# A two-block transformer kernel: the first attention in paired units with four-strip scores, and another way from its output projection into the first feed-forward

## The chip, the cores and the metric

One core of one Trainium2 chip. The metric is the device time in microseconds; lower is better. Engines: TensorE (PE), VectorE (DVE), ScalarE (ACT), GpSimd (POOL), SyncE (SP), which issues the weight loads.

## The reference, cut to what matters

Two transformer blocks on 512 tokens of width 1024, all float32. The change touches the first block's attention and the step from it to the feed-forward:

```python
# 8 heads, two maps each (p), dk = 32, dv = 64; slopes m = 2**-(h+1)
s = einsum('bqhpd,bkhpd->bphqk', q, k) * scale - m * |t - s|
p = softmax(s); w = p[:, 0] - lam * p[:, 1]
attn = rmsnorm(w @ v, g_subln) * (1 - lambda_init)     # mean over the 64 of a head
...
x = x + gt1 * (concat([attn, pool, conv]) @ w_out)
h = rmsnorm(x, g_ffn) * (1 + sc2) + sh2                # modulate
gate, up = split(h @ w_gate_up)
x = x + gt2 * ((silu(gate) * up) @ w_down)
```
`sh2`, `sc2`, `gt2` are columns of `silu(c) @ w_ada + b_ada`.

## The kernel before, in words

Activations lie transposed: width on 128 partitions, 8 chunks k, 512 tokens along the row. Each weight matrix comes in *slabs* of 128 output columns (1024 x 128): SyncE loads the slab into `w_raw` (two slots), ScalarE rounds it to `w_hi` (`split_high`, line 1039), VectorE takes the difference `w_lo` (`split_low`, 1442), TensorE does three matmuls per chunk with the split activations (`three`, lines 517 to 519; `chunk`, `part`, `whole`), 24 of 512 columns a slab. `w_used` counts slabs consumed; slab s+2's rounding waits for slab s. The order on every engine is written out by hand; semaphores carry the rest. PSUM banks have a fixed plan of turns (`plan`, `take`).

*First attention*, 32 units (8 heads x 4 blocks of 128 queries), loop over t. TensorE: scores of unit t, two calls (maps m) of 32 rows (line 635); half of one of the 14 slabs that remain of the input projection; transposes of unit t-2's weights (644); every second t the weighing of the values as `three` of 256 columns with `wt_hi`, `wt_lo`, `v1_hi`, `v1_lo`. VectorE: scores plus the head's ALiBi table with the minimum (1501, reads PSUM), then for unit t-1 reciprocal (1510), scaled second map (1511), combination (1512), for unit t-3 `wt_lo` (1519). ScalarE: exponentials with their sums (1156), `wt_hi` (1142), the output (1149), one ALiBi table a head (1081). GpSimd meanwhile computes, by row products and sums over `w_ada`, the modulation columns SH2 and SC2 (1844, 1846, 1848), and the pool and convolution branches. After the loop follow the pool branch's matmuls, half of two output slabs, the norm over each head (sum on TensorE, root on ScalarE, reciprocal on VectorE), the rest of the output projection.

*From output projection to feed-forward.* Each new chunk of x is squared on ScalarE (1183) and added up by GpSimd in `acc` (1923). After the eighth, TensorE sums over partitions (`token_sums`, 720), ScalarE and VectorE make 1/root, TensorE spreads it over all partitions (`spread`, 729). Then per chunk: `x_scaled` (VectorE, 1590, two buffers), `h_full` and `h_hi` (ScalarE, 1225), `h_lo` (VectorE, `low`, 1448). TensorE runs the gate slab over the eight chunks as they come, and then the up slab (`pair`). At the same time GpSimd makes the GT2 columns (`mod_products`). From then on a pair of gate and up slabs is one step n of 22: silu, product `t_hid`, `hid_hi`, `hid_lo` (1614).

*Second attention*: paired units already, with values weighed in plain float32, 64 columns wide, the two heads of a pair side by side (line 835). It is not touched.

## Time and profile before

| | |
|---|---|
| median of three runs | 1875.13 us (1870.35 to 1875.20) |
| the profiled execution, its own time | 1875.12 us |
| its span, first to last instruction | 1873.2 us |
| TensorE busy | 1765.0 us, 94% |
| VectorE / ScalarE / GpSimd busy | 884.4 / 637.3 / 299.6 us |
| mean granted TensorE clock | 0.970 of full speed |

Times of instructions are counted from the span's start. Matmuls are pipelined: a record's length is longer than the distance to the next one, so rates are read from starts. An idle time in square brackets names what ended it.

### The profile page before, as it was taken

The page shows a single profiled execution, that of the slowest core. Times are in us where ns is not written, and L with a number is a line of the kernel's source. Part 1 is how long each engine was busy: PE and PEld are TensorE (multiplying, and loading weights), DVE is VectorE, ACT ScalarE, POOL GpSimd, SP SyncE. Part 2 cuts the span into 40 slices and gives each one's busy share as a digit, 9 for nine tenths or more (in the row PEclk, how much of TensorE's full clock was granted, in tenths as well). Part 3 has the DMA queues.
Part 4 walks back from the last instruction along what each step waited for, and adds up shares of the span by engine and source line. Part 5 has one row for each costly group of instructions (what it writes and reads, how often), then busy time and mean ns, then how long its engine had stood idle before and what let it go on. Part 6 is the DMA issues. An engine that isn't in the chain of part 4 may idle for free.

```text
span 1873.2 us, 22878 instructions
## 1 busy us (share of the span) xinstructions
PE 1765.0 (94%) x8047; PEld 1399.8 (75%) x8047; DVE 884.4 (47%) x1258; ACT 637.3 (34%) x1088; POOL 299.6 (16%) x237
## 2 busy tenths in 40 slices
PE   5699989699999999999999999899899999999998
PEld 2566667478888887888888887566678888888886
DVE  5678884643333333444443332555545544444322
ACT  3245553422232223222232222354544433233222
POOL 6286621630000112100001012001100200000000
PEclk9799999699999999999999999999999999999999
DMA  9343311333333333533333327111223333333331
GB/s 344 94 135 91 90 34 48 110 112 100 93 98 97 93 98 91 141 93 101 91 108 113 97 87 146 53 50 54 57 79 101 90 91 100 98 92 108 97 96 70
DMA packets 299469, 184.54 MB, mean 99 GB/s; under 512 B 14859, under 2 KB 285703, under 8 KB 299399
## 3 DMA queue, kind: packets, MB, share of 16 engines
q1 hardware_dynamic: 290336, 157.30, 28.6%
q0 software_dynamic: 7424, 25.29, 4.9%
q10 hardware_dynamic: 1656, 1.25, 0.2%
q8 instruction: 33, 0.54, 0.1%
q14 instruction: 20, 0.16, 0.0%
HBM read 180.67 MB, written 6.36 MB: 100 GB/s over the span
## 4 chain that ended last, share of the span: by engine, by line
PE 75%; issue 5%; DVE 3%; ACT 1%; DMA 1%; POOL 1%; DVEq 0%; POOLq 0%; SPq 0%; ACTq 0%
PE psum L517 24%; PE psum L519 24%; PE psum L518 24%; PE psum L862 1%; PE psum L835 1%; DMA w_raw<-in_w_in 1%; PE psum L878 1%; DVE w_lo L1442 1%; DVE h_lo L1448 1%; ACT w_hi L1039 1%; POOL acc L1923 1%; PE psum L729 0%; ACT wt L1325 0%; DVE p L1738 0%; DVE p L1756 0%
## 5 line engine op out<-in xcount | busy, mean ns | idle before, releaser
L517 PE MATMUL psum<-h_hi,w_hi 128*128 128x512 f32 x1480 | 593.0, 401 | 25.1 <-DVE h_lo L1448 11.0
L518 PE MATMUL psum<-h_lo,w_hi 128*128 128x512 f32 x1480 | 582.5, 394 | 0.0
L519 PE MATMUL psum<-h_hi,w_lo 128*128 128x512 f32 x1480 | 582.0, 393 | 0.0
L1442 DVE TENSOR_TENSOR w_lo<-w_raw,w_hi 128x1024 fp32r<-128x1024 f32 (+1 forms) x258 | 365.6, 1417 | 392.1 <-ACT w_hi L1039 388.6
L517 PEld LDWEIGHTS psum<-h_hi,w_hi 128*128 128x128 f32 x1480 | 281.5, 190 | 125.0 <-issue 38.4
L1039 ACT ACTIVATE w_hi<-w_raw 128x1024 fp32r<-128x1024 f32 (+1 forms) x258 | 286.5, 1110 | 161.5 <-PE psum L519 146.5
L519 PEld LDWEIGHTS psum<-h_hi,w_lo 128*128 128x128 f32 x1480 | 281.6, 190 | 60.2
L518 PEld LDWEIGHTS psum<-h_lo,w_hi 128*128 128x128 f32 x1480 | 282.0, 191 | 56.4 <-issue 0.5
L519 PE MATMUL psum<-hid_hi,w_lo 128*128 128x512 f32 x528 | 210.7, 399 | 0.0
L518 PE MATMUL psum<-hid_lo,w_hi 128*128 128x512 f32 x528 | 208.1, 394 | 0.0
L517 PE MATMUL psum<-hid_hi,w_hi 128*128 128x512 f32 x528 | 207.1, 392 | 0.0
L1923 POOL TENSOR_TENSOR acc<-acc,sq 128x512 f32<-128x512 f32 x48 | 65.9, 1373 | 818.7 <-ACT sq L1183 817.8
L1245 ACT ACTIVATE hid_hi<-t_hid 128x512 f32 (+1 forms) x66 | 41.9, 635 | 283.1 <-DVE t_hid L1610 283.1
L518 PEld LDWEIGHTS psum<-hid_lo,w_hi 128*128 128x128 f32 x528 | 99.1, 188 | 25.8
L517 PEld LDWEIGHTS psum<-hid_hi,w_hi 128*128 128x128 f32 x528 | 99.1, 188 | 23.5
L519 PEld LDWEIGHTS psum<-hid_hi,w_lo 128*128 128x128 f32 x528 | 99.1, 188 | 22.8
L1610 DVE TENSOR_TENSOR t_hid<-psum,t_silu 128x512 f32<-128x512 f32 x66 | 45.6, 692 | 141.8 <-PE psum L519 141.8
L1241 ACT ACTIVATE t_silu<-t_gate 128x512 f32<-128x512 f32 x44 | 27.8, 632 | 160.2 <-DVE t_gate L1605 160.2
L1614 DVE TENSOR_TENSOR hid_lo<-t_hid,hid_hi 128x512 f32 (+1 forms) x66 | 47.0, 712 | 64.8 <-ACT hid_hi L1245 64.8
L1848 POOL TENSOR_TENSOR acc<-acc,sq 128x1024 f32<-128x1024 f32 x28 | 75.6, 2699 | 2.2
L1156 ACT ACTIVATE p<-p,stat 128x512 f32<-128x512 f32 x64 | 45.8, 717 | 61.9 <-DVE stat L1501 61.8
L1605 DVE TENSOR_TENSOR t_gate<-psum,rs 128x512 f32<-128x512 f32 x44 | 30.4, 692 | 71.7 <-PE psum L519 71.6
(241 smaller groups left out, 1667.3 us busy)
## 6 DMA issues: line engine op xcount, KB each, us to landing
w_raw<-in_w_in SPq DMA_DIRECT2D x50, 512.0 KB, 3.9
w_raw<-in_w_gate_up SPq DMA_DIRECT2D x44, 512.0 KB, 3.8
w_raw<-in_ffn_w_gate SPq DMA_DIRECT2D x44, 512.0 KB, 3.8
w_raw<-in_ffn_w_up SPq DMA_DIRECT2D x44, 512.0 KB, 3.8
w_raw<-in_ffn_w_down SPq DMA_DIRECT2D x32, 704.0 KB, 4.6
sq<-in_w_ada POOLq DMA_DIRECT2D x32, 512.0 KB, 4.2
w_raw<-in_w_down SPq DMA_DIRECT2D x16, 704.0 KB, 4.6
ada_w<-in_w_ada SPq DMA_DIRECT2D x4, 2048.0 KB, 21.0
```

What stands on the lines that cost most here:

```text
L517: pe.matmul(o, a_hi, b_hi, start=start, stop=False)
L518: pe.matmul(o, a_hi, b_lo, start=False, stop=False)
L519: return pe.matmul(o, a_lo, b_hi, start=False, stop=stop)
L1039: act.activation(w_hi[:, s % 2, 0:n], w_raw[:, s % 2, 0:n], ACT.Identity).then_inc(w_high, 1)
L1156: act.activation(p1[:, t % 3, m, :], p1[:, t % 3, m, :], ACT.Exp, bias=stat[:, t % 3, m:m + 1], scale=-1.0, accum_out=stat[:, t % 3, 2 + m ...
L1245: act.activation(hid_hi[:, slot_of(n, i), :], t_hid[:, :], ACT.Identity).then_inc(hid_high, 1)
L1442: dve.tensor_tensor(w_lo[:, s % 2, 0:n], w_raw[:, s % 2, 0:n], w_hi[:, s % 2, 0:n].bitcast(F32), ALU.subtract).then_inc(w_ready, 1)
L1605: dve.tensor_tensor(t_gate[:, :], psum[:, b, :], rs[:, :], ALU.mult).then_inc(gate_scaled, 1)
L1610: dve.tensor_tensor(t_hid[:, :], psum[:, b, :], t_silu[:, :], ALU.mult).then_inc(hid_set, 1)
L1614: dve.tensor_tensor(hid_lo[:, at, :], t_hid[:, :], hid_hi[:, at, :].bitcast(F32), ALU.subtract)\
L1848: last = pool.tensor_tensor(mod_acc, mod_acc, ada_row[:, k % 2, :], ALU.add)
L1923: pool.tensor_tensor(acc[:, m, :], acc[:, m, :], sq[:, n, m, :], ALU.add).then_inc(summed, 1)
```

## The change

The first attention has 16 units, each a pair of heads and a block of queries. Scores are four calls in four strips of 32 rows, into four banks, issued back to back; all are reduced against one shared distance table `dist` (q carries the reciprocal slope by `qscale`, and the exponential's scale and the small `least` multiply it back). The combination is not normalized: `combine` weighs the second map with -lam times the ratio of sums, and the head norm takes the missing factor by `el` = EPS x sum squared. Weights and values stay plain float32 (`wt`, `v1`) and are weighed in the second attention's manner. p1 has two buffers of four maps instead of three of two. On VectorE `combine(t-1)` stands ahead of unit t's reductions.

Into the feed-forward: slab 29 is split before the root; GpSimd adds seven squares and TensorE sums the eighth from `sq`; `x_scaled` (four buffers) takes `scale2` as well, `h_full` is gone, `h_lo` comes from `x_scaled` plus shift less `h_hi`; gate and up slab run together, chunk by chunk (`first_pair`); GpSimd's GT2 products wait for `hid_ready` 2. The pool branch's second part on ScalarE and VectorE stands at t = 17. The diff, cut:

```diff
         (t_gate, t_silu, t_hid), _ = region(OVER, BIG, [(n, [P, T], F32) for n in ("t_gate", "t_silu", "t_hid")])
-        (x_scaled, h_full), _ = region(OVER + 3 * T * BYTES, BIG, [(n, [P, 2, T], F32) for n in ("x_scaled", "h_full")])
+        (x_scaled,), _ = region(OVER + 3 * T * BYTES, BIG, [("x_scaled", [P, 4, T], F32)])
...
-        (q1, k1, v1_hi, v1_lo, wt_hi, wt_lo, o1, p1, alibi, dist), at1 = region(BIG, BIG_END, [
-            ("q1", [P, 4, T], F32), ("k1", [P, 4, T], F32), ("v1_hi", [P, TT, T], F32R),
-            ("v1_lo", [P, TT, T], F32R), ("wt_hi", [P, 2, TT, 2 * P], F32R),
-            ("wt_lo", [P, 2, TT, 2 * P], F32R), ("o1", [P, 4, T], F32), ("p1", [P, 3, 2, T], F32),
-            ("alibi", [P, 2, 2 * T - P], F32), ("dist", [P, 2 * T - P], F32)])
+        (q1, k1, v1, wt, o1, p1, dist), at1 = region(BIG, BIG_END, [
+            ("q1", [P, 4, T], F32), ("k1", [P, 4, T], F32), ("v1", [P, TT, T], F32),
+            ("wt", [P, 2, TT, 2, 2 * P], F32), ("o1", [P, 4, T], F32), ("p1", [P, 2, 2, 2, T], F32),
...
-                    for m in range(2):
-                        b = take(("s1", t, m))
-                        r = DH * (h % 2) + DQ1 * m
-                        pe.matmul(psum[:, b, :], q1[r:r + DQ1, c, P * i:P * i + P], k1[r:r + DQ1, c, :],
-                                  start=True, stop=True).then_inc(filled[b], 1)
...
-                u = t - 2
-                if 0 <= u < UN1:
-                    pe.wait_ge(combined, u + 1)
...
+                    for j in range(2):
+                        for m in range(2):
+                            take(("s1", t, j, m))
+                    for j in range(2):
+                        for m in range(2):
+                            b = bank_of(("s1", t, j, m))
+                            r = DH * j + DQ1 * m
+                            pe.matmul(psum[:, b, :], q1[r:r + DQ1, c, P * i:P * i + P], k1[r:r + DQ1, c, :],
+                                      start=True, stop=True).then_inc(filled[b], 1)
+                if t < N_MIX1:
+                    part(S_MIX1 + t, 0, 2)
+                u = t - 1
+                if u >= 0:
...
+                    for j in range(2):
+                        pe.wait_ge(combined, 2 * u + j + 1)
+                        b = take(("t1", u, j))
+                        for kt in range(TT):
+                            last = pe.transpose(psum[:, b, P * kt:P * kt + P], p1[:, u % 2, j, 0, P * kt:P * kt + P],
+                                                ident[:, :])
...
-                    wait_emptied(pe, ("t1", 2 * g))
-                    wait_emptied(pe, ("t1", 2 * g + 1))
+                    for j in range(2):
+                        wait_emptied(pe, ("t1", u, j))
...
+                            d = DH * (2 * c + j)
+                            last = pe.matmul(psum[DH * j:DH * j + DH, b, 0:2 * P], v1[:, kt, d:d + DH],
+                                             wt[:, g % 2, kt, j, :], start=kt == 0, stop=kt == TT - 1)
                     last.then_inc(filled[b], 1)
...
-            token_sums("ffn0", "out1")
+            b = take(("sum", "ffn0"))
+            for part_, ready in ((acc[:, 0, :], (summed, SUM0 + KD - 1)), (sq[:, 1, 0, :], (squared, KD))):
+                pe.wait_ge(*ready)
+                for i in range(TT):
+                    last = pe.matmul(psum[:, b, i:i + 1], part_[:, P * i:P * i + P], mean_d,
...
-                pair(0)
+                def first_pair():
+                    for n, key in enumerate(("gate", "up")):
+                        await_slab(s0 + n)
+                        take((key, 0, 0))
+                    for k in range(KD):
+                        pe.wait_ge(h_ready, h0 + k + 1)
+                        for n, key in enumerate(("gate", "up")):
+                            last = three(psum[:, bank_of((key, 0, 0)), :], *tile(s0 + n, k), *hs[k], k == 0, k == KD - 1)
+                            if k == KD - 1:
+                                last.then_inc(w_used, 1)
+                if f == 0:
+                    first_pair()
+                else:
+                    pair(0)
                 pair(1)
...
+            def exps(t, j):
+                c, i = t // 4, t % 4
+                col = 8 * i + 2 * c + j
+                act.wait_ge(least_set, 2 * t + j + 1)
+                for m in range(2):
+                    at = 2 * j + m
+                    act.activation(p1[:, t % 2, j, m, :], p1[:, t % 2, j, m, :], ACT.Exp,
+                                   bias=quad[:, t % 2, 4 + at:5 + at], scale=-(2.0 ** -(2 * c + j + 1)),
+                                   accum_out=lsum[:, m, col:col + 1]).then_inc(expd, 1)
...
-                u = t - 3
+                if t < N_MIX1:
+                    split_high(S_MIX1 + t + 1)
+                if t >= 3 and t % 2:
+                    keep_o1((t - 3) // 2)
...
+                if t < UN1:
+                    exps(t, 0)
+                u = t - 1
...
+                    for j in range(2):
+                        b = wait_filled(act, ("t1", u, j))
+                        act.activation(wt[:, g % 2, :, j, P * (u % 2):P * (u % 2) + P],
+                                       psum[:, b, :].rearrange("p (k q) -> p k q", k=TT), ACT.Copy)\
+                           .then_inc(emptied[b], 1)
...
+                    exps(t, 1)
...
                 act.activation(q1[:, c, :], o1[:, c, :], ACT.Square).then_inc(o_squared, 1)
-            b = wait_filled(act, "sub_sum")
-            act.activation(rsub[:, :], psum[:, b, 0:32], ACT.Sqrt, bias=eps).then_inc(emptied[b], 1)
+            wait_emptied(act, "sub_sum")
+            act.activation(rsub[:, :], rsub[:, :], ACT.Sqrt).then_inc(sub_root, 1)
...
...
                 act.wait_ge(scaled_x, k + 1)
-                if k >= 2:
-                    act.wait_ge(h_ready, 8 * GEN["ffn0"] + k - 1)
-                for dst, done_ in ((h_full[:, k % 2, :], h_whole), (h_hi[:, k, :], h_high)):
-                    act.activation(dst, x_scaled[:, k % 2, :], ACT.Identity, bias=modc[:, SH2 + k:SH2 + k + 1],
-                                   scale=scale2[:, k:k + 1]).then_inc(done_, 1)
+                act.activation(h_hi[:, k, :], x_scaled[:, k % 4, :], ACT.Identity, bias=modc[:, SH2 + k:SH2 + k + 1])\
+                   .then_inc(h_high, 1)
...
-                dve.wait_ge(v_high, i + 1)
-                dve.tensor_tensor(v1_lo[:, i, :], psum[:, b, :], v1_hi[:, i, :].bitcast(F32), ALU.subtract)\
-                   .then_inc(emptied[b], 1)
             split_low(5)
...
+            def combine(u):
+                c, i = u // 4, u % 4
+                at = 8 * i + 2 * c
+                dve.wait_ge(expd, 4 * u + 4)
+                done(dve.reciprocal(quad[:, u % 2, 8:10], lsum[:, 1, at:at + 2]))
+                dve.scalar_tensor_tensor(out=quad[:, u % 2, 10:12], in0=lsum[:, 0, at:at + 2], scalar=neg_lam,
+                                         in1=quad[:, u % 2, 8:10], op0=ALU.mult, op1=ALU.mult).then_inc(ratio_set, 1)
+                dve.wait_ge(ratio_set, u + 1)
+                for j in range(2):
+                    dve.scalar_tensor_tensor(out=p1[:, u % 2, j, 0, :], in0=p1[:, u % 2, j, 1, :],
+                                             scalar=quad[:, u % 2, 10 + j:11 + j], in1=p1[:, u % 2, j, 0, :],
+                                             op0=ALU.mult, op1=ALU.add).then_inc(combined, 1)
...
+                for m in range(2):
+                    wait_emptied(dve, ("s1", t, j, m))
+                dve.tensor_scalar(quad[:, t % 2, 4 + 2 * j:6 + 2 * j], quad[:, t % 2, 2 * j:2 * j + 2],
+                                  2.0 ** -(2 * (t // 4) + j + 1), None, ALU.mult).then_inc(least_set, 1)
...
+                if 1 <= t <= UN1:
+                    combine(t - 1)
+                if t < UN1:
+                    i = t % 4
+                    for j in range(2):
+                        if t >= 2:
+                            wait_filled(dve, ("t1", t - 2, j))
+                        for m in range(2):
+                            b = wait_filled(dve, ("s1", t, j, m))
+                            dve.tensor_tensor_reduce(p1[:, t % 2, j, m, :], psum[:, b, :],
+                                                     dist[:, T - P - P * i:2 * T - P - P * i], 1.0, 3e38,
+                                                     ALU.add, ALU.min, quad[:, t % 2, 2 * j + m:2 * j + m + 1])\
+                               .then_inc(emptied[b], 1)
+                            if j == 1 and m == 0:
+                                least(t, 0)
+                    least(t, 1)
+                if t < N_MIX1:
+                    split_low(S_MIX1 + t + 1)
...
-                    done(dve.reciprocal(st[:, 4:6], st[:, 2:4]))
-                    done(dve.tensor_scalar(p1[:, n, 1, :], p1[:, n, 1, :], st[:, 5:6], neg_lam, ALU.mult, ALU.mult))
-                    dve.scalar_tensor_tensor(out=p1[:, n, 0, :], in0=p1[:, n, 0, :], scalar=st[:, 4:5],
-                                             in1=p1[:, n, 1, :], op0=ALU.mult, op1=ALU.add).then_inc(combined, 1)
...
-                if 0 <= u < UN1:
-                    b = bank[("t1", u)]
-                    at = slice(P * (u % 2), P * (u % 2) + P)
-                    dve.wait_ge(wt_high, u + 1)
-                    dve.tensor_tensor(wt_lo[:, u // 2 % 2, :, at], psum[:, b, :].rearrange("p (k q) -> p k q", k=TT),
-                                      wt_hi[:, u // 2 % 2, :, at].bitcast(F32), ALU.subtract).then_inc(emptied[b], 1)
...
+            dve.scalar_tensor_tensor(out=el[:, :], in0=lsum[:, 0, :], scalar=EPS, in1=lsum[:, 0, :],
+                                     op0=ALU.mult, op1=ALU.mult).then_inc(sub_added, 1)
             split_low(S_OUT1 + 1)
-            wait_emptied(dve, "sub_sum")
+            dve.wait_ge(sub_added, 1)
+            b = wait_filled(dve, "sub_sum")
+            dve.tensor_tensor(rsub[:, :], psum[:, b, 0:32], el[:, :], ALU.add).then_inc(emptied[b], 1)
+            dve.wait_ge(sub_root, 1)
             dve.reciprocal(rsub[:, :], rsub[:, :]).then_inc(sub_scaled, 1)
...
+            split_low(S_GU[0] + 1)
...
-                    if k >= 2:
-                        dve.wait_ge(h_high, 8 * GEN["ffn0"] + k - 1)
-                    dve.tensor_tensor(x_scaled[:, k % 2, :], x[:, k, :], psum[:, b, :], ALU.mult).then_inc(scaled_x, 1)
+                    if k >= 4:
+                        dve.wait_ge(h_ready, 8 * GEN["ffn0"] + k - 3)
+                    dve.scalar_tensor_tensor(out=x_scaled[:, k % 4, :], in0=x[:, k, :], scalar=scale2[:, k:k + 1],
+                                             in1=psum[:, b, :], op0=ALU.mult, op1=ALU.mult).then_inc(scaled_x, 1)
                 if k:
                     j = k - 1
-                    dve.wait_ge(h_whole, j + 1)
-                    low(h_lo[:, j, :], h_full[:, j % 2, :], h_hi[:, j, :], 8 * GEN["ffn0"] + j)
+                    dve.wait_ge(scaled_x, j + 1)
+                    dve.wait_ge(h_high, 8 * GEN["ffn0"] + j + 1)
+                    dve.scalar_tensor_tensor(out=h_lo[:, j, :], in0=x_scaled[:, j % 4, :],
+                                             scalar=modc[:, SH2 + j:SH2 + j + 1], in1=h_hi[:, j, :].bitcast(F32),
+                                             op0=ALU.add, op1=ALU.subtract).then_inc(h_ready, 1)
...
             wait_filled(pool, ("mod", SC2 // KD))
-            sums("out1", None)
+            pool.memset(acc[:, 0, :], 0.0).then_inc(summed, SUM0)
+            pool.wait_ge(summed, SUM0)
+            for n in range(KD - 1):
+                pool.wait_ge(squared, n + 1)
+                pool.tensor_tensor(acc[:, 0, :], acc[:, 0, :], sq[:, n % 2, 0, :], ALU.add).then_inc(summed, 1)
+                pool.wait_ge(summed, SUM0 + n + 1)
+            pool.wait_ge(hid_ready, 2)
             mod_row(GT2 // KD, 0)
-            wait_filled(pool, ("sum", "ffn0"))
             mod_products(GT2 // KD)
             wait_filled(pool, ("mod", GT2 // KD))
-            sums("down0", "ffn0", 2)
+            sums("down0", None, 2)
```

## Rows read from the trace of the kernel before

**Rows 1.** The page: busy time by engine, and the group of slab roundings.
```profile
PE 1765.0 (94%) x8047; PEld 1399.8 (75%) x8047; DVE 884.4 (47%) x1258; ACT 637.3 (34%) x1088; POOL 299.6 (16%) x237
...
L1039 ACT ACTIVATE w_hi<-w_raw 128x1024 fp32r<-128x1024 f32 (+1 forms) x258 | 286.5, 1110 | 161.5 <-PE psum L519 146.5
```
**Rows 2.** Busy time of each engine (instructions) in five stretches, granted clock, DMA.
```profile
105.10:264.20 159.10, 150.24 (x728) 106.14 (x728) 142.67 (x239) 84.82 (x180) 102.39 (x65) 0.97 0.31 91
176.00:218.20 42.20, 38.31 (x189) 27.19 (x188) 40.97 (x60) 21.25 (x46) 38.34 (x21) 0.98 0.41 125
243.00:264.20 21.20, 20.73 (x105) 14.81 (x104) 18.23 (x37) 11.03 (x24) 6.73 (x6) 1.00 0.17 51
...
354.30:376.60 22.30, 13.17 (x25) 6.67 (x25) 22.17 (x15) 13.39 (x17) 20.73 (x13) 0.50 0.30 95
395.90:439.40 43.50, 43.50 (x193) 36.05 (x192) 15.35 (x16) 12.53 (x16) 0.00 (x0) 1.00 0.34 97
```
**Rows 3.** TensorE in time order, two units of the first attention: start us, us.
```profile
171.55 1.13 PE L635 MATMUL psum<-k,q 32*128 32x512 f32 x4
...
172.60 0.50 PE L517 MATMUL psum<-h_hi,w_hi 128*128 128x512 f32 x1
...
175.46 0.60 PE L644 MATMUL psum<-ident,p 128*128 128x128 f32 x4
...
175.99 1.13 PE L635 MATMUL psum<-k,q 32*128 32x512 f32 x4
...
181.86 1.13 PE L635 MATMUL psum<-k,q 32*128 32x512 f32 x4
```
**Rows 4.** TensorE in time order, weighing of values in the second attention.
```profile
1213.04 2.38 PE L835 MATMUL psum<-wt,vb 128*64 128x256 f32 x24
```
**Rows 5.** Time order, units 28 and 29 of the first attention.
```profile
264.22 1.13 PE L635 MATMUL psum<-k,q 32*128 32x512 f32 x4
...
265.52 0.69 DVE L1501 CUSTOM_DVE_ANT_0 p<-psum,alibi 128x512 f32<-128x512 f32 x1 [1.95 <-PE psum L635]
...
266.13 0.68 DVE L1501 CUSTOM_DVE_ANT_0 p<-psum,alibi 128x512 f32<-128x512 f32 x1
266.25 0.72 ACT L1156 ACTIVATE p<-p,stat 128x512 f32<-128x512 f32 x1 [1.54 <-DVE stat L1501]
...
266.94 0.55 DVE L1511 TENSOR_SCALAR p<-p,stat,small 128x512 f32<-128x512 f32 x1
...
267.80 0.60 ACT L1142 ACTIVATE wt_hi<-psum 128x512 fp32r<-128x512 f32 x1
```
**Rows 6.** VectorE's groups, and one line's spread, 176 to 218; last, 243 to 264.
```profile
L1511 DVE TENSOR_SCALAR p<-p,stat,small 128x512 f32<-128x512 f32 x7 | 11.4, 1630 | 0.3
...
L1512 DVE SCALAR_TENSOR_TENSOR p<-p,stat 128x512 f32<-128x512 f32 x7 | 8.8, 1253 | 0.2
...
L1512 DVE SCALAR_TENSOR_TENSOR p<-p,stat x7: 752/753/2747, 180.8 to 217.2; 128x512 f32<-128x512 f32 x7
...
L1442 DVE TENSOR_TENSOR w_lo<-w_raw,w_hi 128x1024 fp32r<-128x1024 f32 x2 | 2.4, 1224 | 1.1 <-ACT w_hi L1039 1.1
```
**Rows 7.** TensorE in time order, start of the second output slab.
```profile
288.82 0.50 PE L517 MATMUL psum<-h_hi,w_hi 128*128 128x512 f32 x1 [0.57 <-DVE w_lo L1442]
```
**Rows 8.** Time order, from the last output slab into the feed-forward.
```profile
346.54 1.87 PE L720 MATMUL psum<-small,acc 128*128 128x1 f32 x8 [3.08 <-POOL acc L1923]
...
351.08 1.29 DVE L1590 TENSOR_TENSOR x_scaled<-x_res,psum 128x512 f32<-128x512 f32 x2 [2.17 <-PE psum L729]
...
376.59 0.80 PE L517 MATMUL psum<-h_hi,w_hi 128*128 128x512 f32 x1 [1.66 <-DVE w_lo L1442]
...
380.34 0.39 PE L517 MATMUL psum<-h_hi,w_hi 128*128 128x512 f32 x1
...
390.34 0.50 PE L517 MATMUL psum<-h_hi,w_hi 128*128 128x512 f32 x1 [0.99 <-DVE w_lo L1442]
...
395.92 0.39 PE L517 MATMUL psum<-h_hi,w_hi 128*128 128x512 f32 x1
```

More of the change, by code:

```diff
@@ L183, in program @@
         stat = place("stat", [P, 3, 8])
+        quad = place("quad", [P, 2, 16])
+        lsum = place("lsum", [P, 2, 32])
+        el = place("el", [P, 32])
+        qscale = place("qscale", [P, 4])
         rsub = place("rsub", [P, 32])
@@ L649, in _ @@
+                if t < N_MIX1:
+                    part(S_MIX1 + t, 1, 2)
+                if u >= 0 and u % 2:
+                    g = u // 2
+                    c = g // 2
                     if g == 0:
```

187 lines of the change are left out of this document (73 added, 114 removed).

## The prediction, made before the changed kernel was run

> **What bounds the kernel now.** I read the page first, then the busy time by stage, then the two changed stretches instruction by instruction. TensorE is busy 94% of the span [rows 1], so a gain must come from fewer TensorE microseconds or from its waits. The stage view [rows 2] separates three cases. In 395.9 to 439.4 eight slabs take 43.5 us: 5.44 us a slab, 0.227 us a matmul of 512 columns; only fewer matmuls would help there, and the change takes none. In the first attention (105.1 to 264.2, 28 of 32 units with 14 slabs) TensorE is busy 150 of 159 us and VectorE 143. While GpSimd works (176 to 218) TensorE has 38.3 of 42.2 us and VectorE is full (41.0); when GpSimd is nearly quiet (243 to 264) TensorE is full. So this loop has two limits taking turns. In 354.3 to 376.6, the change into the feed-forward, TensorE is busy 13.2 of 22.3 us at a granted clock of 0.50 (1.2 GHz) and VectorE is full.
>
> **The loop: TensorE's side.** Before, an even unit lasts 4.44 us (171.55 to 175.99): 1.05 us scores, 2.86 us half a slab, 0.53 us transposes with their switch [rows 3]. The odd unit behind it, with 12 small matmuls for the values, lasts 5.9 us (to 181.86). Two units: 10.3 us. After, one iteration does two units' work:
> - Scores: four calls in four 32-row strips. Two calls in two strips, two passes each, are four records in 1.13 us, and TensorE goes on after 1.05 [rows 3]. No row has four strips. Bounds: 1.05 us (all together) and 2.1 us (two at a time). I take 1.05, because two strips show no cost of sharing.
> - Slab 5.44 us, eight transposes 0.9 us, switches 0.4 us: 7.8 us.
> - Weighing of values, every second iteration: plain float32, 64 columns wide, two heads side by side. The same form in the second attention takes 2.38 us for 24 records, which are 12 passes a head, eight of 256 and four of 128 columns [rows 4]: 2560 columns a head, 0.93 ns each. Eight passes of 256 are 1.9 us.
> Mean iteration: 7.8 + 1.9/2 = 8.7 us against 10.3 for the same work.
>
> **The loop: VectorE and ScalarE's side.** The scaled product, `wt_lo` and `v1_lo` go away, and the ALiBi tables on ScalarE. But combine(t-1) stands before unit t's score reductions, and p1 has two buffers, so a ring forms. From the first reduction of unit t [rows 5]: three reductions at 0.61 us (265.52 to 266.13) and the small `least`, 2.1; two exponentials 1.55 (266.25 to 267.80), 3.65; two copies of transposed weights at under 0.6 us, 4.8; two exponentials, 6.35; reciprocal and product with their waits 0.45; two products of 0.75 us overlapping slightly, 1.35; so 8.15 us until unit t+1's reductions start. Undisturbed, this hides behind TensorE's 8.7.
> GpSimd disturbs it. In 176 to 218 the combining product has a median of 0.75 us, undisturbed, but a mean of 1.25, and its neighbour a mean of 1.63 [rows 6] instead of 0.55 [rows 5]: 1.6 us extra for a pair. Two such products remain in the ring, so a disturbed iteration takes 9.75 us. GpSimd's work is not reduced: 102 us busy in the old loop [rows 2], of some 131 us in the new: share 0.78. Mean ring: 8.15 + 0.78 x 1.6 = 9.4 us, above 8.7: the ring becomes the bound. The Trainium skill ("TensorEngine Tiling (Array Packing)", PSUM Bottleneck) warns of this: after row tiling, emptying PSUM may be the bottleneck. The trace agrees in kind: four reductions, 2.4 us, follow 1.05 us of scores.
> What is queued in this ring: TensorE's transposes wait for combine; behind them stand the second half slab and the weighing; a late weighing also holds the next scores. Over two iterations these shift by some 2 us but add nothing to 9.4.
>
> **Ends of the loop.** Before: scores of unit 28 at 264.22, second output slab's first matmul at 288.82 [rows 5, 7], 183.7 us from the loop's start at 105.1. After: first reduction at 105.1 + 1.3 = 106.4 (1.3 is 264.22 to 265.52); 14 iterations, 131.6; one more ring, 8.2; then combine 8.2, transposes 0.6 and last copy 0.9 with handshakes, weighing 1.9, pool matmuls 1.9 (four passes of 512 columns at the scores' rate), and from their first half on ScalarE's two copies, two roundings, the slab split of 1.1 [rows 1] and VectorE's difference of 1.2 [rows 6], 4.1 beyond them: 17.7. That is 263.9, or 24.9 us earlier. The drain alone is worse than before (27 us from iteration 14 against 24.6), since no slab covers the two last rings. The added hop in the sub-layer norm (VectorE adds `el` before ScalarE's root) costs 0.3. Result: 24.6 us saved. The added hop is estimated from the reciprocal's place in that chain. The eight more memsets lie in VectorE's wait for the first DMA; uncovered they are one-column writes, well under 0.5 us each.
>
> **The change into the feed-forward.** Squares of the last column go to TensorE directly, so eight sum matmuls start where GpSimd's last addition started: 1.3 us sooner than 346.54, and scaling starts at 349.9 instead of 351.08 [rows 8]. The split of slab 29 fits into that chain's waits (cover: the 4.5 us in which VectorE and ScalarE hold only root and reciprocal; uncovered 2.3 us). The old stretch took 22.3 us for eight k, 2.8 each, with three matmuls a k and GpSimd busy throughout [rows 2]. The new k has two products on VectorE, 1.4 us undisturbed, one rounding on ScalarE, and feeds six matmuls, 1.36 us at full clock. x_scaled has four buffers, so VectorE waits for no one after the first. First matmul at 352.4. From a low clock the old kernel needed 3.75 us for nine back-to-back matmuls (376.59 to 380.34) before the rate rose: 1.7 us lost. End of both slabs: 352.4 + 48 x 0.227 + 1.7 = 365.0. Now the price: both slabs are released together, so slab 30 waits for the gate's silu, some 0.6 like the copies of [rows 5], the split 1.1 and the difference 1.2, less 0.5 since the gate ends first: first matmul at 367.4. Slab 31's split hides behind slab 30. Slab 32 starts at 378.3, against 395.92 before: 17.6 us saved.
> The GT2 products move to where `hid_ready` is 2, some 380, and run for about 41 us as before (some 351 to 392: GpSimd is busy 20.7 of 22.3 us with them in [rows 2], and `w_lo` still suffers at 390), now under the steady stream. There the old kernel shows one such stall: slab 31 waits 0.99 us for `w_lo` [rows 8]. Four pairs of 10.9 us fall into it: 4 us lost, with bounds 0 (each difference falls between GpSimd's operations) and 8. GpSimd's queue holds nothing else due before the down projection. The Trainium skill ("SBUF — State Buffer", SBUF: two separate sides) speaks against this move: a VectorE operation with two SBUF inputs is blocked for the whole of a GpSimd operation that reads SBUF. The trace agrees, by the 0.99 us of slab 31.
>
> **Sum.** 24.6 + 17.6 - 4 = 38.2 us. The profiled execution took 1875.12 us (span 1873.2), equal to the median 1875.13, so the forecast is 1837 us.
>
> **Rivals.**
> 1. *TensorE keeps both stretches.* GpSimd's work hardly hits the ring, since only two products are exposed, and no stalls: 14 x 0.7 = 10 and 4 us more, 1823. For it: the median of 0.75 even in the disturbed stretch [rows 6]. Against: the mean. 12%.
> 2. *Strips run two at a time.* TensorE's iteration becomes 9.75, every iteration is at both limits, about 10.1: +10, 1847. For it: no row with four strips. 10%.
> 3. *Low clock through the first pair.* 48 matmuls at 0.42 (nine in 3.75 us) instead of 0.227, less the 1.7: +8, 1845. For it: 354 to 377 ran at 0.50 throughout. Against: TensorE waited for 9 of those 22 us; back-to-back work from 376.59 raised the clock. 9%.
> 4. *GpSimd's lock at its worst.* Both products last until GpSimd's operation ends, 2.75 each, the longest there [rows 6]: ring 12.3 in ten of 14 iterations, +26, 1863. Stalls may double. 7%.
> 5. *The other side: the ring's waits let the clock fall inside the loop.* At 1.2 GHz an iteration's TensorE work is some 16 us, 6.6 more than the forecast; from six such iterations the whole gain is gone, at ten it is 1903, slower than before. For it: the old loop's mean of 0.97 says that it fell at times. Against: that mean came with TensorE 94% busy, and I expect 93%. 3%.
> 6. *The removed matmuls were covered by waits already*, and the transition gain alone comes: 1861. 3%.
> Forecast 56%.
>
> **How the numbers follow.** Within the forecast: loop bounds 8.7 to 10 us an iteration (-10, +8), stalls 0 to 8 us, first pair +-3: 1826 to 1850. The range for 8 in 10 takes in most of rivals 1 to 3 and stops short of 4 and 6: 1822 to 1857. A difference of 0.3% (5.6 us) is about what this measurement can tell. Only rival 5 and the far ends of 4 and 6 together come near 1869: faster 0.96, within 0.3% 0.02, slower 0.02.
>
> **What would show it.** Right: `p` scores as eight records in about 1.15 us; starts of `psum<-k,q` 9 to 10 us apart, shorter where GpSimd is idle; TensorE waiting for `p` of the combining line; second output slab near 264; six matmuls a k near 1.4 us; a 2.4 us gap before slab 30; GpSimd's `acc` products after the second pair, with `w_lo` far above its 1.2 us and stalls near 1 us beside them. Wrong: scores of 2 us, iterations over 11 us, granted clock 0.50 across the loop or the whole first pair, or stalls of over 2 us a pair.

## The result, and where the microseconds went

The changed kernel takes 1856.8 us (median of four runs, 1855.3 to 1857.9) against 1875.2 for the kernel before on the same chip: a ratio of 0.9908, 95% interval 0.9897 to 0.9920, so 17 us or 0.9% faster. The forecast was 1837, with a range of 1822 to 1857. The profiled execution took 1855.3 us, its span 1853.5, 19.7 less than the span before.

The page's row of busy time, to be read beside [rows 1]:
```profile
PE 1734.3 (94%) x7991; PEld 1377.6 (74%) x7991; DVE 854.1 (46%) x1232; ACT 618.1 (33%) x1064; POOL 303.4 (16%) x236
```
TensorE has 30.7 us less to do, and only 19.7 of them left the span: 11 us turned into waits. Four stretches of the changed kernel, busy time by engine as in [rows 2], say where:
```profile
105.10:254.40 149.30, 126.35 (x696) 89.76 (x688) 129.71 (x220) 73.70 (x168) 105.08 (x64) 0.99 0.32 96
254.40:283.30 28.90, 17.06 (x73) 9.61 (x72) 12.35 (x32) 15.45 (x34) 0.00 (x0) 0.70 0.00 1
343.20:366.20 23.00, 18.24 (x73) 14.64 (x74) 14.56 (x20) 10.08 (x13) 0.00 (x0) 0.88 0.18 52
371.60:415.00 43.40, 41.74 (x181) 33.55 (x180) 23.44 (x16) 12.52 (x16) 34.75 (x21) 1.00 0.60 177
```
The first is 14 iterations of the new loop. TensorE idles 23 of 149 us at full clock and VectorE 20: neither is full, which is what a ring of waits looks like. GpSimd is busy 105 us. From the first reduction of unit 0 (105.97) to that of unit 15 (263.92) the mean distance is 10.5 us; 9.4 was forecast. The single distances go with GpSimd: 11.8 to 15.2 us in the five iterations in which it is busy for some 11 us or more, 8.6 and 7.8 us in the two in which it is busy for under 2 (the last two, without any GpSimd work, run into the drain). Since each unit's reductions stand behind the combining products of the unit before, no distance can be shorter than the ring: undisturbed, the ring is at most 7.8 us long, where 8.15 was forecast. The last stretch runs under GT2's products, where TensorE is no longer full.

The same points of the kernel in both traces (us from the span's start; before from [rows 3, 5, 7, 8], and the last from the same two traces):

| point | before | after | gained so far | forecast |
|---|---|---|---|---|
| second output slab | 288.82 | 283.31 | 5.5 | 24.9 |
| scaling of the feed-forward starts | 351.08 | 343.19 | 7.9 | 25.8 |
| first matmul of slab 32 | 395.92 | 371.60 | 24.3 | 42.2 |
| end of the span | 1873.2 | 1853.5 | 19.7 | 38.2 |

The difference stands in the first line: the loop gained 5.5 us instead of 24.9. The steps behind it came out nearly as forecast, within 1.5 us each.

**The loop, operation by operation.** VectorE's lines in the loop of the changed kernel: number, shortest, median and longest duration in ns. L1520 is `least`, L1508 the ratio, L1512 the two combining products, L1507 the reciprocal, L1475 `w_lo`:
```profile
L1520 DVE TENSOR_SCALAR quad<-quad x32: 155/420/2283, 107.8 to 266.6; 128x2 f32<-128x2 f32 x32
L1508 DVE SCALAR_TENSOR_TENSOR quad<-lsum,small,quad x16: 220/774/1593, 114.3 to 270.1; 128x2 f32<-128x2 f32 x16
L1512 DVE SCALAR_TENSOR_TENSOR p<-p,quad x32: 737/754/2979, 115.5 to 271.0; 128x512 f32<-128x512 f32 x32
L1507 DVE RECIPROCAL quad<-lsum x16: 153/166/168, 114.1 to 269.9; 128x2 f32<-128x2 f32 x16
L1475 DVE TENSOR_TENSOR w_lo<-w_raw,w_hi x15: 1210/1212/1226, 112.5 to 282.0; 128x1024 fp32r<-128x1024 f32 x15
```
An operation on two columns needs 0.155 us and takes up to 2.28. Its neighbour, a reciprocal of the same size, takes 0.15 to 0.17 every time. Over all their instances, the time beyond the shortest is 16.6 us for `least`, 9.1 for the ratio and 22.4 for the combining products: 48 us (called blocked time below), of which the forecast had counted 17.5 (14 iterations at 1.25), and only on L1512. That is 3.0 us a unit; with a ring of at most 7.8 it makes 10.8, an estimate to be held against the 10.5 measured. One stretch shows what they wait for and how that reaches TensorE, all engines in time order (start, duration; in brackets the idle time before and what ended it):
```profile
124.25 2.11 DVE L1520 TENSOR_SCALAR quad<-quad 128x2 f32<-128x2 f32 x1
...
124.42 1.91 POOL L1896 TENSOR_TENSOR sq<-sq,cact 128x1024 f32<-128x1024 f32 x1
...
126.28 1.21 DVE L1475 TENSOR_TENSOR w_lo<-w_raw,w_hi 128x1024 fp32r<-128x1024 f32 x1
126.39 0.72 ACT L1140 ACTIVATE p<-p,quad 128x512 f32<-128x512 f32 x1 [0.33 <-DVE quad L1520]
126.40 3.32 POOL L1898 TENSOR_TENSOR acc<-acc,sq 128x1024 f32<-128x1024 f32 x1
...
127.82 0.57 ACT L1120 ACTIVATE k<-psum 128x512 f32<-128x512 f32 x1
...
128.15 1.59 DVE L1508 SCALAR_TENSOR_TENSOR quad<-lsum,small,quad 128x2 f32<-128x2 f32 x1
...
128.54 0.47 PE L522 MATMUL psum<-h_hi,w_hi 128*128 128x512 f32 x1 [2.73 <-ACT k L1120]
...
129.78 3.30 DVE L1512 SCALAR_TENSOR_TENSOR p<-p,quad 128x512 f32<-128x512 f32 x2
...
130.61 1.91 POOL L1896 TENSOR_TENSOR sq<-sq,cact 128x1024 f32<-128x1024 f32 x1
...
132.60 2.74 POOL L1898 TENSOR_TENSOR acc<-acc,sq 128x1024 f32<-128x1024 f32 x1
...
133.13 0.66 PE L653 MATMUL psum<-ident,p 128*128 128x128 f32 x4 [1.15 <-DVE p L1512]
```
`least` ends at 126.36, when GpSimd's multiplication ends (126.33). `w_lo` starts right there, ahead of GpSimd's next operation, and now GpSimd waits: its addition lasts 3.32 us, where the one at 132.60 lasts 2.74 and the one at 104.88, with nothing of VectorE beside it, 2.38. The ratio then waits until 129.74, that addition's end (129.72), and the two combining products take 3.30 us instead of 1.4, the second one held until the multiplication at 130.61 is over. There are two ways from here to TensorE. The short one is the last row: transposes wait for the combining product. The long one is at 128.54: a late `least` makes the exponentials late; the copy of the slab's result out of its only PSUM bank is queued behind them on ScalarE, and the next half slab waits 2.73 us for that bank.

Does TensorE's lateness come back into the ring? All waits of ScalarE and then of VectorE in the 14 iterations say hardly (us in total, times, longest):
```profile
ACT p L1140 <- DVE quad L1520: 71.9, 19, 8.0
```
```profile
DVE quad L1507 <- ACT p L1140: 12.6, 13, 2.0
DVE p L1547 <- PE psum L643: 6.1, 1, 6.1
DVE y_side L1536 <- PE psum L524: 2.6, 1, 2.6
DVE conv_u L1531 <- PE psum L524: 1.0, 1, 1.0
```
The one wait for scores (L643) is that of unit 0, before the loop. From unit 1 to unit 14 no reduction waits for scores and ScalarE never waits for TensorE; 3.6 us before two products of the convolution branch are all that VectorE waits for it. VectorE and ScalarE set the pace, and TensorE follows.

**TensorE's own side** was as forecast. Scores in four strips, a weighing, the last rings and the second output slab:
```profile
176.41 1.14 PE L643 MATMUL psum<-k,q 32*128 32x512 f32 x8
177.49 0.50 PE L522 MATMUL psum<-h_hi,w_hi 128*128 128x512 f32 x1
...
138.13 1.95 PE L670 MATMUL psum<-wt,v 128*64 128x256 f32 x16 [1.58 <-ACT wt L1185]
...
261.93 1.86 PE L643 MATMUL psum<-k,q 32*128 32x512 f32 x8
...
271.14 1.97 PE L653 MATMUL psum<-ident,p 128*128 128x128 f32 x8 [6.33 <-DVE p L1512]
273.84 3.52 PE L670 MATMUL psum<-wt,v 128*64 128x256 f32 x16 [0.73 <-issue]
...
283.31 0.49 PE L522 MATMUL psum<-h_hi,w_hi 128*128 128x512 f32 x1 [0.33 <-DVE w_lo L1475]
```
Eight records in 1.14 us, four strips together, the next matmul 1.08 after the first: four calls cost what two cost in [rows 3]. The weighing takes 1.95. In the drain the granted clock falls (0.70 over the second stretch above, 0.56 from 270 to 278) and the same weighing takes 3.52.

**The change into the feed-forward**, TensorE and the scaling in time order, to be read beside [rows 8]:
```profile
337.23 0.95 PE L751 MATMUL psum<-small,acc 128*128 128x1 f32 x8
...
343.19 1.41 DVE L1635 SCALAR_TENSOR_TENSOR x_scaled<-x_res,scale,psum 128x512 f32<-128x512 f32 x2 [1.81 <-PE psum L743]
...
345.75 0.77 PE L522 MATMUL psum<-h_hi,w_hi 128*128 128x512 f32 x1 [2.68 <-DVE h_lo L1641]
...
360.54 0.50 PE L522 MATMUL psum<-h_hi,w_hi 128*128 128x512 f32 x1 [2.21 <-DVE w_lo L1475]
...
371.60 0.39 PE L522 MATMUL psum<-h_hi,w_hi 128*128 128x512 f32 x1
```
From the scaling's start to slab 32 it is 28.4 us, as forecast (349.9 to 378.3), and 44.8 before. The scaling itself starts 5.6 us after the last residual (337.57) instead of 7.5 (343.63).

### The profile page after: what moved, and what is told of

It reads as the page before. It is cut to its first block, busy times and chain, and to the rows that moved or that the text cites. A ratio compares the mean times of both kernels' runs of the same rounds, so it can differ in the third digit from the quotient of the medians.

```text
span 1853.5 us, 22726 instructions
## 1 busy us (share of the span) xinstructions
PE 1734.3 (94%) x7991; PEld 1377.6 (74%) x7991; DVE 854.1 (46%) x1232; ACT 618.1 (33%) x1064; POOL 303.4 (16%) x236
## 3 DMA queue, kind: packets, MB, share of 16 engines
q10 hardware_dynamic: 1656, 1.25, 0.2%
## 4 chain that ended last, share of the span: by engine, by line
PE 81%; DVE 10%; ACT 4%; issue 3%; DMA 2%; ACTq 0%; DVEq 0%; SPq 0%
PE psum L522 26%; PE psum L524 25%; PE psum L523 25%; DVE p L1512 2%; ACT p L1140 1%; DVE w_lo L1475 1%; DVE first_acc L1449 1%; DVE p L1547 1%; PE psum L869 1%; DMA ada_w<-in_w_ada 1%; ACT w_hi L1073 1%; PE psum L896 1%; DVE quad L1520 1%; DMA w_raw<-in_w_in 1%; PE psum L912 1%
## 5 line engine op out<-in xcount | busy, mean ns | idle before, releaser
L1475 DVE TENSOR_TENSOR w_lo<-w_raw,w_hi 128x1024 fp32r<-128x1024 f32 (+1 forms) x258 | 357.6, 1386 | 388.0 <-ACT w_hi L1073 384.6
L1974 POOL TENSOR_TENSOR acc<-acc,sq 128x512 f32<-128x512 f32 x40 | 55.6, 1391 | 736.4 <-ACT sq L1215 735.5
L1140 ACT ACTIVATE p<-p,quad 128x512 f32<-128x512 f32 x64 | 45.6, 715 | 80.5 <-DVE quad L1520 80.5
```

What stands on the lines that cost most here:

```text
L1140: act.activation(p1[:, t % 2, j, m, :], p1[:, t % 2, j, m, :], ACT.Exp, bias=quad[:, t % 2, 4 + at:5 + at], scale=-(2.0 ** -(2 * c + j + 1 ...
L1475: dve.tensor_tensor(w_lo[:, s % 2, 0:n], w_raw[:, s % 2, 0:n], w_hi[:, s % 2, 0:n].bitcast(F32), ALU.subtract).then_inc(w_ready, 1)
L1974: pool.tensor_tensor(acc[:, m, :], acc[:, m, :], sq[:, n, m, :], ALU.add).then_inc(summed, 1)
```

## Experiments

All ratios are against the kernel before, timed in the same job; the changed kernel's is 0.9908. "Keep" is when ScalarE keeps the last weighed block of values (277.40 in the changed kernel, 286.04 before), which closes the loop and its drain. It and the blocked time were counted in each trace over the lines named above.

**1 and 2: GpSimd made quiet, in the changed kernel and in the one before.** Left out are seven of eight multiplications and the additions for two vectors; the rest of GpSimd's work stays.
```
 for k in range(KD):
     ...
     pool.wait_ge(row_landed[k % 2], rows_loaded[k % 2])
+    if j in (SH2 // KD, SC2 // KD):
+        if k == KD - 1:
+            last = pool.tensor_tensor(mod_acc, ada_row[:, 1, :], cact[...], ALU.mult)
+        continue
```


> The changed kernel, but GpSimd multiplies only the last of the eight row blocks for each of the two vectors that it computes in the first attention (SH2 and SC2); the other seven multiplications and their additions are left out, their transfers stay. So both vectors, and the output, have other values. Theory A (GpSimd's SBUF operations block VectorE's small and wide operations in the ring): the blocked microseconds, 48 over the three lines, nearly vanish; the loop's mean distance falls from 10.6 to 8.7 to 9.0 us, and the kernel becomes 22 to 28 us faster than the changed one, near 1832. Theory B (the order of the ring, combine before the next reductions with two buffers, binds even without GpSimd): distance stays at 10 us or more, under 8 us gained. Theory C (TensorE's clock): distance stays where the granted clock was low, gain under 5 us.

> The kernel before, with the same operations of GpSimd left out (other values in SH2, SC2 and the output). It is the control. Theory A: the old loop has a third p1 buffer and more of TensorE's work to hide behind, so it gains less than the changed one, some 8 to 14 us against 22 to 28. If it gains as much as the changed one, GpSimd's disturbance was no worse for the new ring than for the old one, and A doesn't explain the shortfall.

Measured: 1831.2 us, ratio 0.9772 (0.9751 to 0.9793), so 26 us faster than the changed kernel; keep 254.34. The kernel before, treated alike: 1865.6, ratio 0.9956 (0.9941 to 0.9971), 8 us faster. The lines of `least` and of the combining products, and 124.9 us of the loop by engine, in the first:
```profile
L1520 DVE TENSOR_SCALAR quad<-quad x32: 154/169/657, 108.5 to 243.5; 128x2 f32<-128x2 f32 x32
...
L1512 DVE SCALAR_TENSOR_TENSOR p<-p,quad x32: 737/750/1870, 112.2 to 247.9; 128x512 f32<-128x512 f32 x32
...
105.10:230.00 124.90, 122.20 (x688) 87.88 (x688) 92.74 (x217) 75.25 (x169) 40.50 (x37) 1.00 0.37 116
```
TensorE now is the bound: 122.2 of 124.9 us busy for the 14 slabs, so 8.7 us of work in an iteration of 8.9, and 8.7 is the forecast's figure for its side. Blocked time fell from 48 to 12 us. GpSimd's operations for the two vectors take 26 us from the new kernel and 8 from the old: the new order is more exposed to the same work. It isn't that there was little to block before. Counted alike (15.0 us on line 1511, 11.6 on 1512, 10.0 on `w_lo`), the old loop had 37 us of blocked time against 48. Taking 28 of the 37 away gave back 8 us there; taking 36 of the 48 away gave back 26 here. Between the two quiet kernels lie 34 us, near the 38 that were forecast for the loud ones. Theory A holds in both numbers, C falls (nothing was done to the clock, which is 1.00 here and was 0.99), and B as the only cause falls.

**3 and 4: the two parts of the change apart.** Experiment 3 is the kernel before with the diff's edits from the sum matmuls of `ffn0` on (`x_scaled`, `first_pair`, the GT2 products' place); experiment 4 has all the others.

> The kernel before with only the edits of the change into the feed-forward (sum matmuls of the last column directly, both slabs together, one rounding per k on ScalarE, GT2 products later). If the parts are additive as the two traces suggest: 14 to 16 us faster than before, about 1860. If the attention's part was worth nothing or less: 18 us, all of the change's gain.

> The kernel before with only the edits of the first attention. Additive as the traces suggest: 5 to 7 us faster, about 1869. If this part was in truth worth what the forecast said and the transition nothing: 18 or more. If it is a loss that the transition covers: no change or slower.

Measured: the transition alone 1857.4 us, ratio 0.9919 (0.9896 to 0.9942), 15 us faster. The attention alone 1871.7 over ten runs, ratio 0.9990 (0.9979 to 1.0001): 2 us, and not to be told from nothing by the 0.3% bound. 5 to 7 us were expected, after the 5.5 us that the traces above show at the second output slab; that figure rather overstates this part. The two add up to the whole. So a loop with 24 us less of TensorE's work in it (1740.9 us busy in experiment 4's trace, 1765.0 before) was worth about 2 us, and the transition made nearly all of the gain.

**5: `least` on ScalarE.**
```
-least(t, 0)
 ...
-least(t, 1)                           # on VectorE
 ...
+act.activation(quad[:, t % 2, 4 + 2*j:6 + 2*j], quad[:, t % 2, 2*j:2*j + 2],
+               ACT.Copy, scale=2.0 ** -(2*c + j + 1)).then_inc(least_set, 1)
```


> The changed kernel with `least` (the product of two columns, 32 of them) on ScalarE instead of VectorE, in front of the exponentials. Theory A as the trace tells it (tiny operations wait for GpSimd too): 16.6 us of blocked time leave VectorE, 32 operations of about 0.25 us enter ScalarE's side of the ring; if the block doesn't move to the next operation, the loop gets 6 to 12 us shorter. Rival A2 (the port is held anyway, so the block moves on to the ratio and the combining products): their mean rises and the kernel stays within 3 us. Theory B: within 3 us as well, but with their means unchanged.

Measured: 1850.5 us, ratio 0.9872 (0.9856 to 0.9889), 6 us faster; keep 269.95. ScalarE's form of it, and the two VectorE lines (here L1479 is `w_lo`, L1512 the ratio) that stand next:
```profile
L1139 ACT ACTIVATE quad<-quad 128x2 f32<-128x2 f32 x32 | 6.4, 200 | 65.1 <-DVE quad L1551 65.1
```
```profile
L1479 DVE TENSOR_TENSOR w_lo<-w_raw,w_hi x15: 1212/1216/2942, 107.8 to 275.7; 128x1024 fp32r<-128x1024 f32 x15
...
L1512 DVE SCALAR_TENSOR_TENSOR quad<-lsum,small,quad x16: 220/846/2152, 110.7 to 262.5; 128x2 f32<-128x2 f32 x16
```
On ScalarE it takes 0.200 us every time. But `w_lo`, never blocked in the changed kernel's loop, now goes up to 2.94 us, and the ratio's longest grows from 1.59 to 2.15: of the 16.6 us that left with `least`, 8.3 came back on the next operations. `w_lo` had been free only because `least` had waited in front of it. Both A and A2 hold, each for half.

**6 and 7: a third buffer and another order, alone and with `least` on ScalarE.** The edit in short:
```
-("p1", [P, 2, 2, 2, T], F32)            +("p1", [P, 3, 2, 2, T], F32)
 # VectorE, iteration t
-combine(t - 1); reductions of t; w_lo    +reductions of t; w_lo; combine(t - 1)
 # TensorE and ScalarE
-u = t - 1   # unit transposed, copied    +u = t - 2
```


> The changed kernel with a third p1 buffer; VectorE reduces unit t before it combines unit t-1, and TensorE transposes unit t-2. Everything else stays, GpSimd's work too. Theory B (the ring's order lets each blocked microsecond through to the end): distance falls from 10.6 to 9.0 to 9.6 us, since blocked time fills VectorE's idle time; the end one iteration later takes back 2 to 4; 12 to 20 us faster, about 1840. Theory A alone (VectorE is full with blocked time whatever the order): under 5 us. Theory C (clock): under 3 us.

> Both edits: the third buffer with the other order, and `least` on ScalarE. If both causes count: 3 to 8 us faster than the skewed ring alone. If the skewed ring has already hidden the blocked time behind TensorE: within 2 us of it. If ScalarE's two small operations come late for the exponentials: slower than it by 2 to 4.

Measured: alone 1849.5 us, ratio 0.9861 (0.9844 to 0.9877), 8 us faster, keep 270.05. Together 1839.6 us, ratio 0.9811 (0.9794 to 0.9827), 17 to 18 us faster than the changed kernel, keep 259.58. Alone it gained about half of what theory B wanted (12 to 20 us); together they gained more than was expected (3 to 8 us beyond experiment 6, measured 10). The loop of experiment 6 by engine:
```profile
105.10:249.30 144.20, 129.93 (x672) 92.80 (x665) 127.88 (x213) 73.19 (x165) 102.33 (x64) 0.93 0.33 99
```
The granted clock is 0.93 where it was 0.99 in the changed kernel, and TensorE is busy 129.9 us with fewer matmuls than took 126.4 there. Part of what this experiment lacks may be the clock; nothing here takes the two apart, and the profiled execution was its slowest run (1852.3). TensorE's waits in the loop, the changed kernel first, then the one with both edits (us in total, times, longest):
```profile
PE psum L653 <- DVE p L1512: 9.9, 9, 2.2
PE psum L522 <- ACT k L1120: 5.5, 2, 2.7
```
```profile
PE psum L670 <- ACT wt L1189: 4.5, 3, 3.0
PE psum L653 <- DVE p L1516: 1.8, 3, 1.4
```
The waits for the combining product nearly go. Blocked time does not (44.6 us, against 48): it is now borne beside TensorE's work. In the version with the third buffer alone, `least` still stands in front of `w_lo` and of the exponentials, and the waits for ScalarE's copies behind them stay; that would be the part that `least` on ScalarE then takes. This is a reading, not shown: the 3 to 4 us by which 17 to 18 exceeds the sum of 8 and 6 are as much as single runs of one kernel differ (2 to 4 us), and the clock differs too (0.97 in experiment 7's loop).

**8: GT2's products where they were before.**
```
-pool.wait_ge(hid_ready, 2)
 mod_row(GT2 // KD, 0)
+wait_filled(pool, ("sum", "ffn0"))
 mod_products(GT2 // KD)
```


> The changed kernel, but GpSimd's GT2 products start when the sum matmuls of the scaling have run, as before the change, and not after the first gate-and-up pair. Forecast's reason: the products then lie under the eight k of the transition, where VectorE issues two products a k; the six matmuls a k stretch from 1.4 towards 2.5 us, 5 to 9 us lost there, and 2.9 us of stalls later come back in part: 3 to 7 us slower than the changed kernel. Rival: the transition has room, so the earlier start costs nothing and saves up to 2.9 us.

Measured: 1862.4 us, ratio 0.9930 (0.9910 to 0.9950), 4 to 6 us slower than the changed kernel (its profiled execution, 1864.5, 9 us slower). Its transition in time order:
```profile
345.88 2.70 POOL L1898 TENSOR_TENSOR acc<-acc,sq 128x1024 f32<-128x1024 f32 x1
346.27 0.73 DVE L1635 SCALAR_TENSOR_TENSOR x_scaled<-x_res,scale,psum 128x512 f32<-128x512 f32 x1
...
346.93 2.20 DVE L1641 SCALAR_TENSOR_TENSOR h_lo<-x_scaled,modc,h_hi 128x512 fp32r<-128x512 f32 x1
```
Both products are 512 wide and have the same form. `x_scaled` has one input in PSUM and takes 0.73 us in the middle of GpSimd's addition; `h_lo` has both in SBUF, takes 2.20 and ends 0.55 us after GpSimd's addition (348.58). A k takes 2.8 us here, as in the kernel before. From the scaling to slab 30 it is 29.5 us instead of 17.4; under the steady stream behind it TensorE waits no more. The move was worth its price.

**9: GpSimd's operations in halves.**
```
-done(pool.tensor_tensor(ada_row[:, k % 2, :], ...)); last = pool.tensor_tensor(mod_acc, ...)
+for a in range(2):
+    at = slice(D // 2 * a, D // 2 * (a + 1))
+    ...
+    done(pool.tensor_tensor(ada_row[:, k % 2, at], ...))
+    last = pool.tensor_tensor(mod_acc[:, at], ...)
```


> The changed kernel, but each of GpSimd's multiplications and additions for SH2 and SC2 is two of 512 columns instead of one of 1024: the same data, half the length of one operation, twice the number of gaps. Theory A by length (a blocked operation waits for the GpSimd operation that is running): a wait is about half as long, so of the 48 us of blocked time some 15 to 24 go, and the kernel becomes 8 to 15 us faster than the changed one; the longest `least` falls from 2.3 to about 1.3 us. Rival A3 (after each wait GpSimd's next half blocks again, so the sum of waits is what counts): within 3 us, since GpSimd's busy time grows a little. If GpSimd's own chain gets so long that its vectors come late for TensorE: slower.

Measured: 1846.5 us, ratio 0.9855 (0.9834 to 0.9876), 10 us faster; keep 268.36. `least` and GpSimd's additions in it:
```profile
L1520 DVE TENSOR_SCALAR quad<-quad x32: 155/540/1379, 107.2 to 257.4; 128x2 f32<-128x2 f32 x32
```
```profile
L1902 POOL TENSOR_TENSOR acc<-acc,sq 128x512 f32<-128x512 f32 x27 | 40.5, 1498 | 2.1
```
The longest wait falls with the length of GpSimd's operation, 2.28 to 1.38 us, and the longest combining product from 2.98 to 1.85. Blocked time goes from 48 to 36, somewhat less than expected. GpSimd's work for the two vectors did not shrink, it grew from 65 to 73 us: this ties the wait to the length of one GpSimd operation, not to how much GpSimd does.

**10 to 12: edits together, and the new order without GpSimd.**

> Third buffer with the other order, `least` on ScalarE, and GpSimd's SH2 and SC2 operations in halves. If the causes add: 3 to 8 us faster than the version with the first two (1839.6), about 1834. If the other order has already hidden what is left of the waits: within 2 us of it.

> As the one before, and the GT2 operations under the second and later gate-and-up pairs in halves too. Theory: the differences `w_lo` there wait for half an operation less; of the 2.9 us of stalls 1.5 to 2.9 come back. Rival: a difference in progress delays GpSimd and is delayed the same way, nothing changes (within 1 us).

> Third buffer with the other order, `least` on ScalarE, and GpSimd's operations for SH2 and SC2 left out as in the first experiment (other values in both vectors and the output). It says what the order of the ring costs without GpSimd. Theory A: it cost nothing, so this is within 3 us of the first experiment (1831.2, distance 8.9). Theory B: 5 us or more below it, since TensorE no longer waits for `combined` at all.

Measured: 10, 1841.2 us, ratio 0.9821 (0.9803 to 0.9840), no better than experiment 7: the halves add nothing to the other two edits. 11, 1838.0, ratio 0.9803 (0.9785 to 0.9821), 3 us below 10. Its `w_lo` under the GT2 products, after the changed kernel's over the same slabs:
```profile
L1475 DVE TENSOR_TENSOR w_lo<-w_raw,w_hi x10: 1212/1686/3416, 374.3 to 425.0; 128x1024 fp32r<-128x1024 f32 x10
```
```profile
L1479 DVE TENSOR_TENSOR w_lo<-w_raw,w_hi x10: 1226/1924/2504, 361.0 to 409.3; 128x1024 fp32r<-128x1024 f32 x10
```
The longest is 0.9 us shorter, and that suffices: from the first matmul of one slab pair to that of the next it is 10.88 us undisturbed; the four disturbed pairs of the changed kernel took 11.65, 11.83, 11.78 and 11.18, here 11.11, 10.94, 10.88 and 10.88. Experiment 11 beats both kernels: 2.0% faster than the kernel before. 12, 1826.5, ratio 0.9746 (0.9724 to 0.9768): 5 us below experiment 1. So the two edits are worth 5 us even without GpSimd's two vectors, and these cost 26 us in the changed order (the changed kernel against experiment 1) but 12 to 13 in the new one (experiment 7 against 12).

## Why the forecast was wrong, step by step

The gain was 17 us where 38 were forecast. 1856.8 still lies within the stated range, at its very end; the sum deserves no credit for that, since an iteration of the loop took 10.5 us, outside the 8.7 to 10 from which the forecast was built.

- **TensorE's side of the loop**: right. Four strips in 1.05 to 1.1 us, weighing 1.95 (forecast 1.9), 8.7 us of work an iteration, and that much is measured once GpSimd is quiet. Rival 2 is out.
- **The ring of 8.15 us, and that it would become the bound**: right. Undisturbed it is at most 7.8 us, so 8.15 was a little long; TensorE waits for the combining product (9.9 us, nine times) and idles while VectorE idles too.
- **"Two such products remain in the ring"**: this is the step that failed. The disturbance was counted on the two 512-wide products alone, and for them it was right in size: 22.4 us over 16 units is 1.4 a unit, forecast 1.25. The two `least` and the ratio stand in the same ring and wait as long, since a wait is as long as the rest of GpSimd's operation, not as the waiting one: another 25.7 us, 1.6 a unit. So the mean ring came to 10.5 us and not 9.4, and unit 15's reductions started at 263.92 where the sum has 246.2: 17.7 of the 19.4 us that are missing at the second output slab. The forecast gave `least` its place in the ring but no wait; it priced it by its size. Removing GpSimd's work (1), this operation (5) or half the length of the waits (9) gave back 26, 6 and 10 us; the forecast's price for all of GpSimd's disturbance of the loop was 10 (its rival 1). The Trainium skill ("SBUF — State Buffer", SBUF: two separate sides) says which operations are open to this: a VectorE operation in a two-port mode, or one with two SBUF inputs while GpSimd's reads SBUF too, shares one pair of ports with GpSimd, and whichever starts first holds it for its whole length. The trace agrees, with 2.28 us for two columns; the forecast had used the rule for `w_lo` and not gone down the list of the ring's own operations with it.
- **How a late ring reaches TensorE**: incomplete, but without harm to the sum. Beside the transposes, the slab's single PSUM bank is freed by a copy behind the exponentials on ScalarE: 5.5 us in two waits for `k` alone. The forecast's "these shift by some 2 us but add nothing" holds as far as TensorE's waits go: between units 1 and 14 only 3.6 us of VectorE's time waited for TensorE.
- **The drain**: 17.7 us from the last unit's reductions, measured 19.4 (263.92 to 283.31); transposes and weighing ran there at the low clock and took 1.97 and 3.52 us instead of 1.03 and 1.95. The forecast had them at full speed.
- **The transition**: right. The direct sum matmuls brought 1.8 us (1.2 to 1.3 forecast), first matmul 2.6 us after the scaling (2.5), 28.4 us to slab 32 (28.4), the gap before slab 30 2.2 us (2.4). The low clock ended inside the first pair (granted clock 0.50 from 345.7 to 348, 1.00 from 350 on): rival 3 is out, and experiment 3 finds 15 us for this part with GT2's price in it, against 13.6 forecast (17.6 less 4).
- **GT2 under the steady stream**: mechanism right, 2.9 us lost by the four distances above (forecast 4, bounds 0 to 8); placing them earlier costs more (8).
- **The rivals**: in outcome it is rival 6, the transition's gain alone (1861 against 1856.8), but not by its reason: the removed matmuls had not been covered by waits, since 34 us lie between the two kernels once GpSimd is quiet in both, of which the transition makes some 15 (experiment 3) and leaves some 19, an estimate, to the loop. In cause it is rival 4, GpSimd's lock (1863), but that too spoke only of the two products, at their longest; the end comes from more operations at their mean. Rival 5 did not occur: the clock was 0.99 in the loop (though 0.93 in experiment 6's).
- **What stays open**: the ratio was not taken off VectorE, so its share of the 26 us is not measured by itself. Experiments 6 and 7 suggest, and do not show, that order and `least` support each other; how much of experiment 6's small gain is the clock; how the remaining 13 us between experiments 7 and 12 divide among ratio, `w_lo` and combining products was not tried.

## What to carry to other kernels

When a change shortens the work beside a ring of waits, list every VectorE operation in that loop with its input places, however small, and add to each the rest of a GpSimd operation, by the share of time that GpSimd is busy; operations with an input in PSUM, the reciprocal, and ScalarE's were not held here. Taking one such operation away gives back only part, since the next one on the queue meets the same GpSimd operation; together with one more buffer and an order by which the wait falls beside TensorE's work, it gave 17 to 18 us. And a removed matmul is worth something only where TensorE bound before and still binds after: the attention's part here brought 2 us as the kernel stood. How long the blocked operations last in all says little about the price: removing 28 us of it gave the old kernel 8, removing 36 us the new one 26. What counts is whether the wait stands in the ring that sets the pace.

## What the runs showed of the hardware

- A VectorE operation on 128x2 elements, 0.155 us by itself, took up to 2.28 us beside GpSimd's 1.9 to 2.7 us operations, and up to 1.38 when those were half as wide. The reciprocal of 128x2 between them never took over 0.17, the reduction out of PSUM 0.69, ScalarE's exponential 0.73.
- It works both ways: when `w_lo` (1.21 us) starts in the gap before GpSimd's addition, this takes 3.30 to 3.32 us (five of five times), against 2.38 with nothing of VectorE beside it.
- Four float32 calls in four strips of 32 rows, 512 columns each, run in 1.08 us together; two calls in two strips took 1.05.
